# The FFN of a decoder step as seven half-size products, its inner operands kept in DRAM

## The reference, cut to what matters

```python
def sq_relu_mlp(h, w1, w2):
    return jnp.square(jax.nn.relu(h @ w1)) @ w2

x = x + sq_relu_mlp(rmsnorm(x, P['norm_ffn_g'][l]), P['w_ff1'][l], P['w_ff2'][l])
...
return rmsnorm(x, P['norm_f_g']), ...
```

## Time and profile before

| | |
|---|---|
| median of 3 runs | 2332.1 us (2331.18 to 2332.59) |
| the profiled execution | 2333.0 us; span of its instructions 2331.2 us |
| TensorE busy | 2270.8 us, 97% of the span, 13504 matmuls |
| weight loads (PEld, beside the matmuls) | 2210.0 us, 95% |
| VectorE (DVE) busy | 892.9 us, 38% |
| ScalarE (ACT) busy | 424.1 us, 18% |
| GpSimd (POOL) busy | 788.1 us, 34% |
| DMA | 165.7 MB, 71 GB/s over the span |

### The profile page before, as it was taken

The page is one execution under the profiler, slowest core; times in us unless marked ns, Lnnn a source line. Parts: engine busy times, 40 slices in busy tenths (PEclk is TensorE's granted clock), DMA queues, the critical chain, the costliest instruction groups (busy, mean ns, idle before and its releaser), DMA issues.

```text
span 2331.2 us, 32659 instructions
## 1 busy us (share of the span) xinstructions
PE 2270.8 (97%) x13504; PEld 2210.0 (95%) x13504; DVE 892.9 (38%) x1019; ACT 424.1 (18%) x646; POOL 788.1 (34%) x623
## 2 busy tenths in 40 slices
PE   6999999999999999999999999999999999999997
PEld 5998899999999999999999866999999999999997
DVE  5558898651212212123562641563112212211213
ACT  4322222212110110111110630121001101100113
POOL 6114100004444444444544110443333333333331
PEclk9999999999999999999999999999999999999999
DMA  6522432223121121112110343111111111111122
GB/s 204 149 75 77 131 120 87 66 74 113 51 64 60 55 65 55 55 45 107 51 45 28 109 140 114 46 38 44 46 45 45 46 45 42 39 45 45 37 63 77
DMA packets 199950, 165.71 MB, mean 71 GB/s; under 512 B 6200, under 2 KB 179256, under 8 KB 199847
## 3 DMA queue, kind: packets, MB, share of 16 engines
q1 hardware_dynamic: 182614, 136.31, 19.4%
q10 hardware_dynamic: 16993, 28.12, 3.5%
q0 software_dynamic: 256, 0.01, 0.0%
HBM read 141.88 MB, written 23.02 MB: 71 GB/s over the span
## 4 chain that ended last, share of the span: by engine, by line
PE 93%; DVE 3%; ACT 1%; issue 1%; DMA 1%; POOL 0%; ACTq 0%; DVEq 0%; POOLq 0%
PE PS L707 84%; PE PS L1087 1%; PE PS L1049 1%; PE PS L738 1%; DVE slots_d L1697 1%; PE PS L1020 1%; PE PS L769 1%; PE PS L1005 1%; PE PS L1062 1%; DMA xring<-in_x_prompt 1%; DVE w_lo L1720 0%; PE PS L817 0%; PE PS L784 0%; PE PS L1034 0%; PE PS L925 0%
## 5 line engine op out<-in xcount | busy, mean ns | idle before, releaser
L601 POOL TENSOR_TENSOR w_hi<-w_raw,ones 128x512 fp32r<-128x512 f32 x278 | 312.8, 1125 | 1265.1 <-PE PS L707 1218.7
L605 POOL TENSOR_TENSOR w_lo<-w_raw,w_hi 128x512 fp32r<-128x512 f32 x278 | 392.7, 1413 | 21.8
L707 PE MATMUL PS<-h_hi,w_hi 128*128 128x364 f32 x1512 | 337.9, 332 | 5.6 <-DVE w_lo L1720 5.2
L707 PE MATMUL PS<-h_hi,w_lo 128*128 128x364 f32 x1512 | 334.4, 330 | 0.0
L707 PE MATMUL PS<-h_lo,w_hi 128*128 128x364 f32 x1512 | 334.4, 330 | 0.0
L707 PEld LDWEIGHTS PS<-h_hi,w_hi 128*128 128x128 f32 x1512 | 261.2, 189 | 11.5 <-issue 9.7
L707 PEld LDWEIGHTS PS<-h_hi,w_lo 128*128 128x128 f32 x1512 | 263.0, 188 | 0.0
L707 PEld LDWEIGHTS PS<-h_lo,w_hi 128*128 128x128 f32 x1512 | 263.0, 188 | 0.0
L707 PE MATMUL PS<-mv_hi,w_hi 128*128 128x364 f32 x1104 | 244.6, 330 | 0.0
L707 PE MATMUL PS<-mv_lo,w_hi 128*128 128x364 f32 x1104 | 243.6, 329 | 0.0
L707 PE MATMUL PS<-mv_hi,w_lo 128*128 128x364 f32 x1104 | 243.6, 329 | 0.0
(11 more groups left out here) (260 smaller groups left out, 2356.0 us busy)
## 6 DMA issues: line engine op xcount, KB each, us to landing
w_raw<-in_w_in SPq DMA_DIRECT2D x64, 512.0 KB, 4.2
w_raw<-in_w_ff SPq DMA_DIRECT2D x64, 512.0 KB, 4.0
branch_scratch<-oring ACTq DMA_DIRECT2D x16, 544.0 KB, 3.1
xring<-in_x_prompt SPq DMA_DIRECT2D x16, 512.0 KB, 5.5
w_raw<-in_w_branch SPq DMA_DIRECT2D x16, 512.0 KB, 3.5
kvring<-in_cache_mem_k SPq DMA_DIRECT2D x8, 1024.0 KB, 5.0
kvring<-in_cache_mem_v SPq DMA_DIRECT2D x8, 1024.0 KB, 4.9
tmp<-branch_scratch ACTq DMA_DIRECT2D x12, 544.0 KB, 3.6
```

The lines of the kernel that those rows point to most:

```text
L601: nc.gpsimd.tensor_tensor(w_hi[:, z % 2, cols], w_raw[:, z % 2, cols], ones[:, 0:1].broadcast_to([P, 512]), ALU.mult).then_inc(w_hi_done, 1)
L605: nc.gpsimd.tensor_tensor(w_lo[:, z % 2, cols], w_raw[:, z % 2, cols], w_hi[:, z % 2, cols].bitcast(F32), ALU.subtract).then_inc(w_split, 1)
L707: mm = mmul(acc[:, c, 0:cw], w, r[:, kt, c0:c0 + cw], start=(kt == 0 and e == 0), stop=(kt == kts - 1 and e == 2))
```

## The change

The FFN's two matrix products are done in 2 x 2 blocks by a scheme with seven block products instead of eight (Strassen's in Winograd's form). A block splits the output rows in two, the inner dimension in two (even and odd tiles of 128) and the tokens in two halves of HT = 544. A *unit* makes 256 output rows for all tokens by the seven products P1, P6, P2, P7, P5, P3, P4, in this order.

- **Phase 1**, 16 units (U1), makes all of the hidden layer; its inner dimension is 1024, so a product has 4 pairs of tiles. **Phase 2**, 32 units, goes in 8 chunks of 512 hidden channels, 4 units each; a product has 2 pairs. Each product has 3 terms and two matmuls of 272 columns per pair and term. A product writes one of four bank pairs (three in the first unit and the last four).
- **Weights.** Both phases need five sums of weight blocks and seven low parts per unit, on GpSimd (`add`, `weight_lo`); seven high parts on ScalarE (`weight_hi`). Each is 128 x 512 in phase 1 and 128 x 256 in phase 2. The raw weights are 1 MB in phase 1 (`raw1`, one buffer, loaded when the last low part of the unit before is made) and 0.5 MB in phase 2 (`raw2`, two buffers). The slots for the split blocks are single in phase 1, double in phase 2.
- **Products out of PSUM.** ScalarE copies P1 (`p1_copied`); VectorE combines the others (`p6_added`, `hidden_11` to `hidden_21`), and in phase 2 adds them to x.
- **Moving operands.** Those of phase 1 are made in the attention output stage and at the start of unit 0. For phase 2 the seven combinations of the hidden blocks are made in f32 after each phase-1 unit (`hidden_sums`), stored to a DRAM scratch (`unit_store`, 1.95 MB), reloaded chunk by chunk (`operand_load`, 0.56 MB each) and split by ScalarE and VectorE (`operand_hi`, `operand_lo`, 128 x 1088). x itself is stored to DRAM before the FFN (`x2_dram`) and reloaded at the start of phase 2, since its place holds the stage of the hidden blocks.
- **The end.** The transposes of x's tiles stand in the last three units; the last two tiles' come after the last product, in two groups of tokens (tiles 5 to 8, then 0 to 4).

The diff, cut to its core:

```diff
+def slot_free(u, p):
+    last = u - 1 if u <= U1 else max(u - 2, U1 - 1)
+    return done(last, p)
...
+        def raw_load(u):
+            if u == 0:
+                sp.wait_ge(*split_done(S_FF - 1))
+            else:
+                sp.wait_ge(w_op_lo, 7 * (u if u <= U1 else max(u - 1, U1)))
...
+            sp.dma_start(dst, src).then_inc(w_in_dram[u % 2], 16)
+        raw_load(0)
+        for u in range(U1):
+            raw_load(u + 1)
+            if u >= 1:
+                unit_store(u - 1)
+        raw_load(U1 + 1)
+        for k in range(3):
+            operand_load(0, k)
+        sp.wait_ge(x2_out, 16 * KT)
+        sp.wait_ge(*unit_stored(U1 - 2))
+        for i in range(2):
+            residual_load(i)
+        for k in range(3, 7):
+            operand_load(0, k)
+        raw_load(U1 + 2)
+        unit_store(U1 - 1)
+        sp.wait_ge(*unit_stored(U1 - 1))
+        for i in range(2, KT):
+            residual_load(i)
...
-        with pool.Fori(0, (S_END - S_XO) // 2) as i:
+        with pool.Fori(0, (S_FF - S_XO) // 2) as i:
...
+        def weight_lo(u, p):
+            pool.wait_ge(w_op_hi, done(u, p))
+            if p == 6:
+                pool.wait_ge(w_sums, 4 * u + SUM_OF[3])
+            add(slot_lo(u, p), w_source(u, p), slot_hi(u, p).bitcast(F32), ALU.subtract).then_inc(w_op_lo, 1)
+        for u in range(U_ALL):
...
+            add(sums_tmp(u, 0), a21, a11, ALU.subtract).then_inc(w_sums, 1)
+            weight_lo(u, 1)
...
+            add(slot_f32(u, 6), sums_tmp(u, 0), a22, ALU.add).then_inc(w_sums, 1)
+            add(sums_tmp(u, 1), a12, slot_f32(u, 6), ALU.subtract).then_inc(w_sums, 1)
+            weight_lo(u, 6)
+            weight_lo(u, 2)
+            weight_lo(u, 7)
...
+            add(slot_f32(u, 5), a21, a22, ALU.add).then_inc(w_sums, 1)
+            weight_lo(u, 5)
+            weight_lo(u, 3)
+            weight_lo(u, 4)
...
+            for k, p in enumerate(ORDER):
+                pe.wait_ge(w_op_lo, 7 * u + k + 1)
+                bank_free(u, k)
+                for j in range(js):
+                    operand_ready(u, p, j)
+                    for e, (w, x) in enumerate(((wh, xh), (wh, xl), (wl, xh))):
+                        for c in range(2):
+                            mm = mmul(PS[:, 2 * BANKS[u, k][0] + c, 0:HC], w, x[:, HC * c:HC * c + HC],
+                                      start=(j == 0 and e == 0), stop=(j == js - 1 and e == 2))
+                mm.then_inc(wino, 1)
...
+        for u in range(U1 + 1):                      # ScalarE
+            if u >= 1:
+                weight_hi(u, 3)
+                hidden_squared(u - 1, "h21")
+                weight_hi(u, 4)
+                p1_copied(u)
+            if u == U1:
+                break
+            weight_hi(u + 1, 1)
+            weight_hi(u + 1, 6)
+            hidden_squared(u, "h11")
+            weight_hi(u + 1, 2)
...
+            weight_hi(u + 1, 7)
+            hidden_squared(u, "h22")
...
+            weight_hi(u + 1, 5)
+            hidden_squared(u, "h12")
...
+        def scaled_relu(dst, half):                  # VectorE
+            r = tmp[0][:, HALVES[half]]
+            v.scalar_tensor_tensor(out=dst, in0=dst, scalar=0.0, in1=r, op0=ALU.max, op1=ALU.mult)
+        def hidden_sums(u):
+            v.tensor_tensor(hidden(u, 7), h12, h22, ALU.subtract)
+            v.tensor_tensor(hidden(u, 5), h12, h11, ALU.subtract)
+            v.tensor_tensor(hidden(u, 6), h22, hidden(u, 5), ALU.subtract)
+            v.tensor_tensor(hidden(u, 4), hidden(u, 6), h21, ALU.subtract)
+        for u in range(U1, U_ALL):
+            if u > U1:
+                p6_added(u)
...
+            v.tensor_tensor(two(x11), product_of(u, 2), two(x11), ALU.add).then_inc(taken, 1)
+            v.tensor_tensor(x11, x11, s1, ALU.add).then_inc(s1_used, 1)
+            p7_added(u)
+            v.tensor_tensor(two(x22), product_of(u, 5), two(x22), ALU.add)
+            v.tensor_tensor(two(u4), product_of(u, 5), two(u2), ALU.add).then_inc(taken, 1)
+            v.tensor_tensor(x22, x22, u3, ALU.add)
+            v.tensor_tensor(x21, x21, u3, ALU.add).then_inc(c21_part, 1)
+            v.tensor_tensor(two(x12), product_of(u, 3), two(x12), ALU.add).then_inc(taken, 1)
+            v.tensor_tensor(x12, x12, u4, ALU.add).then_inc(c12_out, 1)
+            v.tensor_tensor(two(x21), two(x21), product_of(u, 4), ALU.subtract).then_inc(taken, 1)
+            if chunk_of(u) + 1 < CHUNKS2:
+                for k in ((), (0, 1, 2), (3, 4), (5, 6))[f % PAIRS]:
+                    operand_lo(chunk_of(u) + 1, k)
```

More of the change, by code:

```diff
@@ L8 @@
+import itertools
 from contextlib import ExitStack
@@ new lines, in _, with bank_free @@
+        product(N_XO + 6, S_XO + 6, mv_hi, mv_lo)
+        product(N_XO + 7, S_XO + 7, mv_hi, mv_lo, used=moving_used)
+        def bank_free(u, k):
+            b, before = BANKS[u, k]
+            if before is None:
+                if u == 0:
+                    n = N_XO + (6 if b == 0 else 7)
+                    pe.wait_ge(drained[n % 2], n // 2 + 1)
+                else:
+                    pe.wait_ge(aux_drained, AUX["sum1s"] + 1)
+            elif before[1] == 0:
+                pe.wait_ge(s1_ready, before[0] + 1)
+            else:
+                pe.wait_ge(taken, 6 * before[0] + before[1])
@@ new lines, in p1_copied, with hidden_squared @@
+        def p1_copied(u):
+            act.wait_ge(wino, done(u, 1))
+            if u == 0:
+                act.wait_ge(sumsq, 10 + KT)
+            else:
+                act.wait_ge(s1_used, u)
+            copy(two(s1), product_of(u, 1)).then_inc(s1_ready, 1)
+        def hidden_squared(u, block):
+            src, p, count = {"h11": (u4, 1, 4 * u + 1), "h22": (hidden(u, 3), 3, 4 * u + 2),
+                             "h12": (hidden(u, 5), 5, 4 * u + 3), "h21": (u3, 2, 4 * u + 4)}[block]
+            act.wait_ge(h_relu, count)
+            if u < 2:
+                act.wait_ge(late_lo, len(LATE))
+            else:
+                act.wait_ge(*unit_stored(u - 2))
+            nc.scalar.activation(hidden(u, p), src, ACT.Square).then_inc(h_sq, 1)
@@ new lines, in operand_hi @@
+        def operand_hi(c, k):
+            p = ORDER[k]
+            act.wait_ge(*operand_in(c, p))
+            copy(opnd[p][:, chunk_rows(c), 0, :], opnd[p][:, chunk_rows(c), 1, :].bitcast(F32)).then_inc(h_op_hi, 1)
+        for i in range(N_LATE_EARLY, N_LATE_EARLY + 3):
+            late_operand_hi(i)
+        p1_copied(0)
+        for i in range(N_LATE_EARLY + 3, N_LATE_EARLY + 6):
+            late_operand_hi(i)
+        weight_hi(0, 3)
+        weight_hi(0, 4)
+        for i in range(N_LATE_EARLY + 6, len(LATE)):
+            late_operand_hi(i)
@@ L1588, in y_squares @@
+        for k in range(4, 7):
+            operand_hi(0, k)
         def y_squares(part, tiles):
@@ new lines, in _ @@
+        inverse_rms(1, None)
+        p7_added(0)
+        root_inverted(1, HALVES[0])
+        hidden_22_added(0)
+        dve.wait_ge(r_ready, 2)
+        scaled_relu(u4, 0)
+        root_inverted(1, HALVES[1])
+        dve.wait_ge(r_ready, 3)
+        scaled_relu(hidden(0, 3), 1)
+        for u in range(U1 + 1):
+            if u >= 1:
+                hidden_21(u - 1)
+                hidden_sums(u - 1)
+                p6_added(u)
+            if u == U1:
+                break
+            if u > 0:
+                hidden_11(u)
+            if u == U1 - 1:
+                operand_lo(0, 0)
+                operand_lo(0, 1)
+            if u > 0:
+                p7_added(u)
+                hidden_22(u)
+            if u == U1 - 1:
+                operand_lo(0, 2)
+                operand_lo(0, 3)
+            hidden_12(u)
```

655 lines of the change are left out of this document (484 added, 171 removed).

## The result

The changed kernel takes 2355.6 us (median of 4 runs, 2353.1 to 2358.5) against 2332.4 us: a ratio of 1.0098, 95% interval 1.0081 to 1.0116. It is slower by 23 us, where 128 were forecast. The profiled execution has a span of 2356.7 us and a time of 2358.5.

A forecast was written before the change was run, and what follows sets the result against it. TensorE, 97% busy, bounded the kernel; afterwards GpSimd and VectorE's shared SBUF access would. Old time less old FFN, plus phase 1, phase 2 and edges: 2333 - 768 + 421 + 467 + 15 = 2468; forecast 2460 us, range 2330 to 2610.

The forecast's parts named there:

- The clock did not fall: Rival: TensorE's pauses drop its clock to the 1.2 GHz level in every product; about 2810 us, chance 0.04.
- no queue made units of 30 and 17 us: Rival: in-order queues of ScalarE and VectorE tie engines together, units over 30 and 17 us; 2604 us, chance 0.06.
- Units of 24 to 28 and 13 to 16 us: Sign of being right: phase-1 units of 24 to 28 us, TensorE waiting for low parts; phase-2 units of 13 to 16.
- GpSimd's operations in phase 1 at a mean of 1.6 us or more: Sign of being right: GpSimd's 512-element operations lengthened to this mean, against 1.29 us undisturbed.
- VectorE's SBUF operations of 544 elements at over 1 us: Sign of being right: these lengthen beside GpSimd, while VectorE's PSUM operations stay at 0.72 us.
- 16 x (26.3 - 23.73): Phase-1 term: 26.3 us a unit from DMA, GpSimd's operations, waits and VectorE's share; 421 us for 16 units.
- 32 x (14.6 - 11.94): Phase-2 term: 14.6 us a unit from GpSimd's and VectorE's SBUF operations added, plus waits; 467 us for 32 units.
- Edges: Start 4 us, change between the phases 4 (0 to 10), tail 7 more (3 to 10): 15 us in the sum.
- Per unit GpSimd now does 12 two-input operations (five sums, seven low parts): GpSimd's count per unit: 15.5 us in phase 1 at 1.29 each, 9.0 in phase 2 at 0.75.
- So the durations of these two kinds must be added.: GpSimd's and VectorE's two-SBUF-input operations never overlap; phase 2: 9.0 + 2.9 + 2.26 = 14.2 us a unit.
- Phase 1's collisions, 4.5 us: Of VectorE's 6.0 us of SBUF operations per phase-1 unit, 1.5 may fall into GpSimd's DMA gap; 4.5 add to the chain.
- with the issue 5.3: Phase-1 weight load in GpSimd's chain: the 1024 KB slab lands in 5.0 us, 5.3 with the issue, every unit.

The follow-up runs named there:

- lockfree: Changed kernel with VectorE's operations with two SBUF inputs replaced by one-input reductions from unit 2 on (leaves work out): 2288.3 us.
- the run with twelve: Changed kernel with sum 3 made twice in every unit, so GpSimd has 12 two-input operations and not 11: 2400.1 us.
- latestore: Changed kernel with the 1.9 MB store of a phase-1 unit held back until sum 7 of the next unit has begun to use the slab: 2343.6 us.

## Why the forecast was wrong in size

**Right.** The mechanism, the direction, and TensorE's 126 ns a matmul. GpSimd's operations and VectorE's with two SBUF inputs hold each other up, those that read PSUM don't; lockfree shows what that is worth. The clock did not fall, and no queue made units of 30 and 17 us.

**Missed, of its own signs.** Units of 24 to 28 and 13 to 16 us: they took 23.73 and 11.94. GpSimd's operations in phase 1 at a mean of 1.6 us or more: 1.46 (1.28 to 1.55 by group). VectorE's SBUF operations of 544 elements at over 1 us: 1.19 in phase 1, but 0.95 in phase 2. The time lay inside the stated range, 2330 to 2610; what failed are terms of the sum.

**Where the 109.5 us went** (sum 2468, profiled time 2358.5). Phase 1: 16 x (26.3 - 23.73) = 41 too many. Phase 2: 32 x (14.6 - 11.94) = 85 too many. Edges: 2358.5 - (2333 - 768 + 380 + 382) = 31.5 where 15 stood, 16.5 too few. 41 + 85 - 16.5 = 109.5.

1. *"Per unit GpSimd now does 12 two-input operations (five sums, seven low parts)".* There are four sums (of P7, P6, P3 and P5); the code counts `w_sums` by 4 a unit, and the description of the change has the same slip. Worth 44 us by the run with twelve. This failed step could have been avoided without a chip.
2. *"So the durations of these two kinds must be added."* The sign is right, the price is not, and with 32 x 1.8 = 58 us it is the largest term. The forecast put all 5.2 us of VectorE's SBUF operations on GpSimd's chain in phase 2; they cost it 3.1. The earlier trace rows show single collisions of long operations, where the excess was the rest of the other's operation to 0.15 us. With short operations back to back each collision cost a quarter of a microsecond less than the other's duration (0.49 of 0.72, 1.04 of 1.29), which is 1.1 us over the 4.75 collisions of a unit. And only 3.25 of the 4 short ones and 1.5 of the 1.75 long ones held GpSimd up, which is 0.9. By the forecast's rule, with 11 operations, a phase-2 unit has 8.1 + 5.2 + 0.4 = 13.7 us; with the measured collisions it is 8.1 + 3.25 x 0.49 + 1.5 x 1.04 + 0.6 idle = 11.9, and 11.94 was measured. Why a quarter of a microsecond isn't paid no run shows. The Trainium skill ("SBUF — State Buffer", section "Summary: rules for kernel authors") has the second instruction to issue wait until the first has finished. The rows of this case say a quarter of a microsecond less.
3. *Phase 1's collisions, 4.5 us.* They took 1.9, 3.9 collisions of 0.48: of VectorE's eight SBUF operations a unit the forecast put six on the chain, and four held GpSimd up. 16 x 2.6 = 42 us. Lockfree, without them, gives 1.7 us a unit. Where the others fell isn't separated; the slab's load, in which they cost GpSimd nothing, was longer than forecast.
4. *The slab, "with the issue 5.3".* GpSimd stood 6.9 us for it, so this term was 16 x 1.6 = 26 us too small. 1.1 of the 1.6 is the 1.9 MB store issued 1.4 us behind the slab, as latestore shows; the rest is open. In a phase-1 unit points 1, 3 and 4, and waits of 0.8 where 1.0 stood, give -1.3 - 2.6 + 1.6 - 0.2 = -2.5 us; measured were 2.6 less.
5. *Edges.* The change of phase cost 11.4 (forecast 4): units 15 to 19 took that much more than their kind. The end cost 11.2 (7), and units 40 to 46 took 4.3 more than their kind, which wasn't forecast. The start has what is left of the 31.5, some 5 (4). At the change of phase I looked for late data and not at what stands behind the wait: VectorE's low halves ahead of P7, with TensorE's banks behind P7.

With only point 1 put right the sum would have been about 2424, with only the collisions of both phases about 2369 (2468 - 16 x 2.6 - 32 x 1.8).

What stays open: which order of operations a phase-2 unit would need to stay clear of collisions. With none it would be TensorE's 10.55 us; the complete kernels reached 11.79. The shares of points 2 and 3 between fewer collisions and cheaper ones are read from the trace; no run sets them apart.

## What to carry to other kernels

A new stage must be counted from the code, operation by operation, before it is multiplied by 48. Where two engines hold each other up, price a collision from rows of operations as short and as dense as the new ones, not by the sum of two durations, and test the design once with the collisions taken out: it says at once what rearranging can be worth. A single buffer whose load stands in the chain of a busy engine is paid in every round; loading it in two parts, as its readers finish, was worth more here (42 us) than the whole change had lost (23).

## What was not expected of the hardware

A VectorE operation of 544 elements with two SBUF inputs held GpSimd up for 0.49 us, not for its 0.72, and one of 1088 for 1.04, not 1.29. The 1024 KB slab landed in 5.7 us with the store held back (latestore) and in 6.8 with a 1.9 MB store issued 1.4 us behind it on the same queue: here the later transfer slowed the earlier one.
